# A two-block network in fp32 on one core: `work` and `small` allocated right behind `x`, `h` and `hh`

## The reference

```python
x = x + 0.5 * gate * ((silu(h @ w_gate) * (h @ w_up)) @ w_down)   # 4 times, D_FF = 2816
x = x + gate * ssd_mixer(h, ...)       # once;   h @ w_in, scan, @ w_out
x = x + gate * mla_mixer(h, ...)       # once;   latent attention
x = x + g1 * mix                       # twice;  rwkv7 + pooling
act = gelu(h2 @ u.T)                   # twice;  16384 experts, u and v are 16384 x 1024
x = x + g2 * ((weights * act) @ v)
```

## The kernel before

| tensor | start | modulo 1024 | modulo 128 |
|---|---|---|---|
| line_half (8 bytes) | 16512 | 128 | 0 |
| ring | 16544 | 160 | 32 |
| weights_hi | 32928 | 160 | 32 |
| arena (with more_lo at 80032) | 49312 | 160 | 32 |
| line_rest (8 bytes) | 180384 | 160 | 32 |
| x, h, hh | 180416, 188608, 196800 | 192 | 64 |
| vfirst, cols | 204992, 209088 | 192 | 64 |
| kept, zeros | 211744, 213792 | 800 | 32 |
| eps, modc | 214048, 214144 | 32, 128 | 32, 0 |
| one_minus_k_a | 215104 | 64 | 64 |
| work, small | 215136, 223328 | 96 | 96 |
| ident_bf16 | 228448 | 96 | 96 |

## Time and profile before

### The profile page before, as it was taken

The page is one execution under the profiler, slowest core; times in us unless marked ns, Lnnn a source line. Parts: engine busy times, 40 slices in busy tenths (PEclk is TensorE's granted clock), DMA queues, the critical chain, the costliest instruction groups (busy, mean ns, idle before and its releaser), DMA issues.

```text
span 3423.6 us, 68787 instructions
## 1 busy us (share of the span) xinstructions
PE 3283.2 (96%) x26804; PEld 3139.6 (92%) x26804; DVE 2585.0 (76%) x4576; ACT 1610.8 (47%) x2594; POOL 197.3 (6%) x331
## 2 busy tenths in 40 slices
PE   6999989999999998999999999998899999999998
PEld 5999769999967997989999999998789999999998
DVE  7989667989836896747878867776846977877776
ACT  3456644454445445134454444544315444444444
POOL 1100001111100110200000000000300000000000
PEclk9999999999999999999999999999999999999999
DMA  9965218979612983045765577775215765567775
GB/s 373 369 226 167 74 50 332 379 282 373 262 42 95 398 313 123 20 154 182 224 209 166 167 236 232 237 233 165 67 55 176 227 216 181 168 200 234 236 240 183
DMA packets 246578, 707.46 MB, mean 207 GB/s; under 512 B 27472, under 2 KB 93008, under 8 KB 244928
## 3 DMA queue, kind: packets, MB, share of 16 engines
q1 hardware_dynamic: 212112, 571.64, 49.3%
q0 software_dynamic: 34224, 132.46, 10.2%
HBM read 669.40 MB, written 34.60 MB: 206 GB/s over the span
## 4 chain that ended last, share of the span: by engine, by line
PE 80%; DMA 8%; DVE 6%; ACT 3%; issue 2%; SPq 0%; DVEq 0%; POOL 0%; ACTq 0%; POOLq 0%
PE psum L516 35%; PE psum L549 25%; DMA ring<-stream 6%; PE psum L1073 3%; PE psum L895 2%; PE psum L1008 1%; PE psum L646 1%; DVE ring L1640 1%; ACT weights_hi L1145 1%; PE psum L915 1%; PE psum L497 1%; PE psum L528 1%; PE psum L529 1%; DVE arena L1698 1%; PE psum L730 1%
## 5 line engine op out<-in xcount | busy, mean ns | idle before, releaser
L516 PE MATMUL psum<-hh,weights_hi 128*128 128x256 f32 x4216 | 1199.4, 284 | 25.0 <-DVE ring L1640 13.6
L1145 ACT ACTIVATE weights_hi<-ring 128x1024 fp32r<-128x1024 f32 x711 | 753.7, 1061 | 970.4 <-DMA ring<-stream 913.3
L1640 DVE TENSOR_TENSOR ring<-ring,weights_hi 128x1024 fp32r<-128x1024 f32 x711 | 871.7, 1228 | 422.4 <-ACT weights_hi L1145 418.5
L516 PE MATMUL psum<-h,weights_hi 128*128 128x256 f32 x4216 | 1182.4, 280 | 0.0
L516 PE MATMUL psum<-hh,ring 128*128 128x256 f32 x2976 | 834.4, 280 | 0.0
L516 PEld LDWEIGHTS psum<-hh,weights_hi 128*128 128x128 f32 x4216 | 797.4, 189 | 35.1 <-DVE ring L1640 19.9
L516 PEld LDWEIGHTS psum<-h,weights_hi 128*128 128x128 f32 x4216 | 797.7, 189 | 0.2
L549 PE MATMUL psum<-small,weights_hi 128*128 128x256 f32 x2752 | 768.0, 279 | 3.6 <-DVE work L2115 1.6
L549 PE MATMUL psum<-work,weights_hi 128*128 128x256 f32 x2752 | 763.8, 278 | 0.0
L549 PE MATMUL psum<-small,ring 128*128 128x256 f32 x2304 | 639.5, 278 | 0.0
L516 PEld LDWEIGHTS psum<-hh,ring 128*128 128x128 f32 x2976 | 564.0, 190 | 0.0
(11 more groups left out here) (410 smaller groups left out, 3901.6 us busy)
## 6 DMA issues: line engine op xcount, KB each, us to landing
ring<-stream SPq DMA_DIRECT2D x735, 512.0 KB, 4.1
arena<-mod_weights POOLq DMA_DIRECT2D x224, 512.0 KB, 6.6
arena<-stream SPq DMA_DIRECT2D x222, 512.0 KB, 6.1
acts<-small SPq DMA_DIRECT2D x256, 128.0 KB, 2.3
work<-acts SPq DMA_DIRECT2D x256, 128.0 KB, 3.0
arena<-cond_rows POOLq DMA_DIRECT2D x3, 1024.0 KB, 7.2
arena<-w_uq POOLq DMA_DIRECT2D x1, 3072.0 KB, 10.8
arena<-constants POOLq DMA_DIRECT2D x2, 1200.0 KB, 5.7
```

The costliest lines, as they stand in the source:

```text
L516: mm = pe.matmul(out, lhs[:, d, :], rhs[:, d, :], start=(d == 0 and p == 0), stop=(d == DT - 1 and p == 2))
L1145: act.activation(whi[:, NTH[n] % WS, :], raw(n), ACT.Copy).then_inc(sem["block_hi"], 1)
L1640: dve.tensor_tensor(low(n), raw(n), whi[:, NTH[n] % WS, :].bitcast(F32), ALU.subtract)\
```

## The change

The two allocations of `work` and `small` move from behind `one_minus_k_a` to right behind `hh`; the unused 8-byte tensor in front of `ring` gets another name; the unused tensor behind the arena becomes 16 bytes instead of 8. The change is described as putting x, h, hh, work and small all at 24 modulo 1024 with the weights 8 bytes up; the kernel's text says nothing of addresses, these follow from the order and the allocator's rounding. No instruction is added, removed or moved.

```diff
-        sb("line_half", [P, 2])
+        sb("ahead_of_weights", [P, 2])
         ring, (ring_lo,) = sb_twice("ring", [P, RING, 1024], [([P, RING, 1024], F32R)])
...
         sb("arena_high", [P, 128 - 30 - 4 * MORE, 256])
-        sb("line_rest", [P, 2])
+        sb("behind_weights", [P, 4])
         x = sb("x", [P, DT, T])
-
         h, (h_lo,) = sb_twice("h", [P, DT, T], [([P, DT, T], F32R)])
         hh, (h_hi,) = sb_twice("hh", [P, DT, T], [([P, DT, T], F32R)])
+        work, (_, gat_lo) = sb_twice("work", [P, 2048], [([P, 1024], F32), ([P, 4, T], F32R)])
+
+        small, (gat_hi, _) = sb_twice("small", [P, 5, T], [([P, 4, T], F32R), ([P, T], F32)])
         vfirst = sb("vfirst", [P, 4, T])
...
         omk = sb("one_minus_k_a", [P, 8])
 
-        work, (_, gat_lo) = sb_twice("work", [P, 2048], [([P, 1024], F32), ([P, 4, T], F32R)])
-
-        small, (gat_hi, _) = sb_twice("small", [P, 5, T], [([P, 4, T], F32R), ([P, T], F32)])
```

## The result

The changed kernel takes 3425.64 us (median of 15 runs, 3422.33 to 3430.82); the kernel before, in 15 runs of its own, 3418.77 us (3410.49 to 3425.49). The ratio is 1.0022, 95% interval 1.0014 to 1.0031: slower, by 6.9 us, where 1.0060 (20.5 us) was forecast. The direction came out as predicted, and so did the new pace of the matmuls; the size is a third of the forecast.

The account below looks back on a forecast made before the run. TensorE, busy 96%, was taken as the bound: matmul count times distance between starts. FFN 5.5 + `v` products 13.2 - stops 2 = +16.7 us, raised to 20 on the 3415.5 us median: 3436 us, range 3411 to 3447.

Parts of the forecast that it names:

- the price of line 549 by line 516's pace: FFN down products: 2112 matmuls go from 114.46 to 117.06 ns each, +5.5 us.
- The products with `v`: Line 549's matmuls in two stages, 3072 each, slow to 117.06 ns: +4.6 and +8.6, +13.2 us.
- The stops: Short TensorE halts in the `v` stages, some 6 us each; slower matmuls give the feeding loop time: -2 us.
- I therefore add 20 us to the median: Whole kernel: typical runs have fewer slow spells than the profiled one and lose more, so 20 us instead of 16.7.
- The other uses of `work` and `small` I cost at nothing: VectorE operations, activation transfers and one-hot products on these tensors: 0 us; the one-hot operands' distance stays 0.
- The 0.9 us that the prediction set as the bound for the transfers of stored activations: Transfers from and to `small` and `work` could lose at most TensorE's waits for `work` in a `v` stretch.
- The pace as the loop's own: Line 549 keeps 113.4 ns whatever its addresses: 3415 us, chance 0.18.
- A better place for line 549: Line 549 keeps 113.4 ns and is freed from the slow pace: 11 us less, 3404 us, chance 0.06.
- rival 3: The new place is worse for line 549, 120 ns: +43 us, 3458 us, chance 0.05.
- Packing by 8 bytes: Addresses come out packed by 8 bytes as described, so the main loop's own distance changes; chance 0.01.
- The reading behind the price: Matmul loops of lines 516, 549, 813: a period saved per float of distance, 120.0, 116.7 and 113.4 ns.
- The rule of the Trainium skill that the prediction weighed: TensorE's independent read ports never wait on anyone, so no start address could matter: 0 us.

Follow-up runs that it names:

- before_c: The kernel before, unchanged, run a third time for another trace; no time of its own given, the kernel before has 3418.77 us.
- all_96: Changed kernel with `cols`, `zeros`, `one_minus_k_a` and a 32-byte pad ahead of `x`, moving operands at 96 modulo 1024: 3395.24 us, 0.9932 of the kernel before.
- all_256: Changed kernel with a 64-byte pad ahead of `x`, moving operands at 256 modulo 1024: 3477.17 us, 1.0181 of the kernel before.
- all_224: Changed kernel with a 32-byte pad ahead of `x`, moving operands at 224 modulo 1024: 3436.65 us, 1.0051 of the kernel before.
- weights_192: Changed kernel with `ahead_of_weights` enlarged, weights and moving operands all 32 bytes up, distances kept: 3427.61 us, 1.0030 of the kernel before.

## Why the prediction was right in direction and too large

- **The addresses, and the price of line 549 by line 516's pace**: right. FFN down pieces in three traces each: before (228.01 + 228.00 + 225.88) / 3 = 227.30 us, after 233.00 three times, for 1992 matmuls; for all 2112 that is 5.70 x 2112 / 1992 = +6.0 us. Forecast: +5.5.
- **The products with `v`**: +13.2 - 2 was forecast, +2 x 2.7 = +5.4 us came (means 356.7 and 359.4 us). This is the step that failed most: the term was mis-sized. The steady pace after was right, 116.95 ns for 117.06. Before, it was 115.42 over six stages, while I had priced it from two of them as (718 - 12) / 6144 = 114.9; the second, with 19 of 128 blocks slow, was the luckiest of six (19 to 96). That is 1.5 ns for 2.2, and 9.4 us for 13.2. The stops fell from 4.9 to 2.9 us a stage (stage time less its blocks at their steady pace): -4 where I had -2.
- **"I therefore add 20 us to the median"**: wrong, 3.3 us more than the sum of 16.7 gave (3.8 with the rounding to 3436). I read the profiled execution's 10 us over the median as slow spells of line 549 and took other runs to have fewer. The repeats have more of them, 139 and 164 for 101. That execution was long in the stages of `u` instead: 202.1 + 205.5 us for the 70 blocks against 198.2 + 197.9 in before_c, 11.5 us.
- **"The other uses of `work` and `small` I cost at nothing"**: wrong by the one-hot part, 2 x 1.4 = -2.8 us. I had argued that line 1073's own distance stays 0. What the move changed is the pace in which line 516 goes on behind it.
- **The sum** of what the traces show: 6.0 + 5.4 - 2.8, and -2.0 from the 70 blocks, which is within their scatter, = +6.6 us, for 6.9 between the medians. On the way from the 20.5 us forecast the `v` term takes away 5.8, the shift to the median 3.8, the one-hot part 2.8 and the 70 blocks 2.0, and the FFN adds 0.5. That the sum comes so near to the measured 6.9 us is in part luck: the stages of `v` scatter from 354.0 to 359.5 us before and from 357.3 to 360.3 after, so by my estimate from these six and six the 5.4 us is known to some 2 us.
- The 0.9 us that the prediction set as the bound for the transfers of stored activations is TensorE's wait for VectorE's writes to `work`, not a wait for a transfer. The term stayed small all the same: no wait of TensorE for a transfer stands among the waits of the first stage of `v`, before or after.
- **The rivals.** The pace as the loop's own: refuted by all_96. A better place for line 549: slow blocks fell in number (84, 110, 58 for 101, 139, 164), but the 3.3 ns of the rest outweigh them. The 120 ns of rival 3 came at +96, not here. Packing by 8 bytes: the addresses exclude it.
- **The reading behind the price**, a period for each float of distance, or the start modulo 128, held only for the three places that it was read from. It gave the right pace here because the new place was one of them; as a law of the place it was luck. For a place not yet seen it would have been wrong: +96 gave 120.0 ns, +128 118.6 or 120.0, +160 117.4 or 118.6, and -32 118.3.
- The rule of the Trainium skill that the prediction weighed ("SBUF — State Buffer", on who interferes with whom: independent read ports for the moving operand and the weight load) would have had all places alike. By all_96 against all_256 the place of the moving operands is worth 82 us, so as it stands it does not describe this stream of float32r weight loads and matmuls.

What makes a stream take 117.8 ns instead of its own pace stays open. In the six traces of the two kernels the pace changed 204 times between blocks, 201 times across a stop and three times across an interval of 125 to 137 ns; most stops changed nothing. The place bears on the share of slow blocks (in line 516 123 and 116 of 527 in two traces of all_96, 498 in all_224, none in all_256) but does not fix it: at +32, in the 419 blocks outside the one-hot parts, it was 65, 98 and 64 in the kernel before, 52, 111 and 62 in the changed one and 9 in weights_192. No run here shows what in the array or the memory does it, nor why the pace follows the distance at all.

## What to carry to other kernels

Where back-to-back matmuls bound a kernel, look at the built addresses and at the distance between starts: the same instructions ran at 113.3 to 120 ns by the place of their operands alone. Against the kernel before, this change with a pad of 160 bytes ahead of `x` gained 0.5% (all_352), and with three tensors and a pad of 32 bytes there 0.7% (all_96). The one mixture of two distances that was tried cost more than either, so first try all moving operands of a stream at one distance from the weights, and check the allocator's rounding before believing a pad. A price read from one trace, of something that falls by chance into one of two paces, needs the same stage in several traces first.

## What the hardware showed that I had not expected

- Distance from weights to moving operands modulo 256 bytes, and the pace of 128x128 weights against 256 float32r columns at a granted clock of 1.00: 0: 120.0 ns (line 813), 32: 116.7 and at times 117.8, 64: 117.8 and seldom 113.3, 96: 120.0, 128: 118.6 or 120.0, 160: 117.4 or 118.6, 192: 113.3 and at times 117.8, 224: 118.3. Steps under 32 bytes were not tried.
- Moving operands at two distances: +32 and -64 in one stream gave 118.9 ns in 312 of 344 blocks with two of three at +32, and 120.0 in 270 of 344 with one of three, slower than either alone.
- A stream resumed behind eight fp32 one-hot products from `work` at distance -64 ran at 117.8 ns, with line 516 itself at +32; with `work` at +32 and at +96 it ran at 116.7. With both at -64 (all_96) it ran at 113.3.
